# The add of the down product to x, per token tile: one operation of 1024 columns in place of two of 512

## What is computed

```python
def layer_tail(x, o_a, o_b, lp):
    o = jnp.concatenate([rmsnorm(o_a, lp['out_norm_a']), rmsnorm(o_b, lp['out_norm_b'])], axis=-1)
    x = x + o @ lp['w_out']
    h = rmsnorm(x, lp['norm2_g'])
    return x + (jax.nn.silu(h @ lp['w_gate']) * (h @ lp['w_up'])) @ lp['w_down']
```

## Time and profile before

| | |
|---|---|
| timed runs, median of 3 | 1887.27 us (1881.82 to 1888.38) |
| the profiled execution | 1884.58 us |
| its span, first to last instruction | 1882.6 us |
| TensorE busy | 1776.3 us, 94% |
| VectorE busy | 728.5 us, 39% |
| ScalarE busy | 390.3 us, 21% |
| GpSimd busy | 273.5 us, 15% |
| L1923, adds of the down product | 396 operations, 251.7 us |
| DMA | 94.73 MB, mean 50 GB/s |

### The profile page before, as it was taken

The page is one execution under the profiler, slowest core; times in us unless marked ns, Lnnn a source line. Parts: engine busy times, 40 slices in busy tenths (PEclk is TensorE's granted clock), DMA queues, the critical chain, the costliest instruction groups (busy, mean ns, idle before and its releaser), DMA issues.

```text
span 1882.6 us, 25099 instructions
## 1 busy us (share of the span) xinstructions
PE 1776.3 (94%) x9317; PEld 1356.1 (72%) x9317; DVE 728.5 (39%) x1319; ACT 390.3 (21%) x862; POOL 273.5 (15%) x286
## 2 busy tenths in 40 slices
PE   7999999698778899999999899999999999999996
PEld 4464454587346666687776698998998998998894
DVE  2100334222224444574565215335335334334437
ACT  2100111122112323332332222112112112112112
POOL 2210121211300000000000113113113112112112
PEclk9999999698967999999999999999999999999999
DMA  8220100533630000000000121211211211211202
GB/s 294 78 89 0 45 1 6 141 90 109 188 107 4 4 4 1 4 4 1 4 1 1 34 68 34 68 33 33 67 33 33 67 33 33 67 33 33 67 11 90
DMA packets 91320, 94.73 MB, mean 50 GB/s; under 512 B 6353, under 2 KB 74546, under 8 KB 91154
## 3 DMA queue, kind: packets, MB, share of 16 engines
q1 hardware_dynamic: 69410, 73.99, 12.8%
q0 software_dynamic: 4240, 11.32, 2.0%
q10 hardware_dynamic: 17600, 8.47, 1.7%
HBM read 86.61 MB, written 11.34 MB: 52 GB/s over the span
## 4 chain that ended last, share of the span: by engine, by line
PE 86%; DVE 5%; issue 3%; DMA 2%; ACT 1%; SPq 1%; ACTq 1%; POOL 0%; POOLq 0%; DVEq 0%
PE bankpair L338 14%; PE bankpair L1793 9%; PE bankpair L1795 9%; PE bankpair L1794 9%; PE bankpair L1452 7%; PE bankpair L1421 6%; PE bankpair L1820 5%; PE bankpair L1511 5%; PE bankpair L1821 5%; PE bankpair L1822 5%; PE bankpair L819 3%; PE bankpair L1490 2%; DMA work<-in_state_win_kv 1%; PE bankpair L1408 1%; PE bankpair L803 1%
## 5 line engine op out<-in xcount | busy, mean ns | idle before, releaser
L1793 PE MATMUL bankpair<-h2T_high,w_high 128*128 128x344 f32 x1056 | 337.9, 320 | 0.0
L1795 PE MATMUL bankpair<-h2T_high,w_low 128*128 128x344 f32 x1056 | 337.1, 319 | 0.0
L1794 PE MATMUL bankpair<-h2T_low,w_high 128*128 128x344 f32 x1056 | 337.1, 319 | 0.0
L338 PE MATMUL bankpair<-work 128*128 128x512 f32 (+3 forms) x720 | 288.2, 557 | 0.8 <-DMA work<-in_w_in 0.8
L1923 DVE TENSOR_TENSOR x_all<-x_all,bankpair 128x512 f32<-128x512 f32 (+1 forms) x396 | 251.7, 684 | 1.7
L338 PEld LDWEIGHTS bankpair<-work 128*128 128x128 f32 (+1 forms) x720 | 127.2, 180 | 145.5 <-issue 136.6
L1909 DVE TENSOR_TENSOR kT_space<-kT_space,bankpair 128x344 f32<-128x344 f32 x66 | 33.9, 513 | 451.4 <-ACT kT_space L1857 451.4
L1793 PEld LDWEIGHTS bankpair<-h2T_high,w_high 128*128 128x128 f32 x1056 | 198.6, 188 | 3.1 <-issue 0.2
L1794 PEld LDWEIGHTS bankpair<-h2T_low,w_high 128*128 128x128 f32 x1056 | 198.1, 188 | 1.1 <-issue 0.2
L1795 PEld LDWEIGHTS bankpair<-h2T_high,w_low 128*128 128x128 f32 x1056 | 198.4, 188 | 0.0
L1844 POOL TENSOR_TENSOR w_low<-work,w_high 128x1024 fp32r<-128x1024 f32 x44 | 105.5, 2421 | 565.5 <-ACT w_high L1839 565.5
(11 more groups left out here) (270 smaller groups left out, 2064.3 us busy)
## 6 DMA issues: line engine op xcount, KB each, us to landing
work<-in_w_gate SPq DMA_DIRECT2D x22, 512.0 KB, 5.0
work<-in_w_up SPq DMA_DIRECT2D x22, 512.0 KB, 6.2
work<-in_w_down SPq DMA_DIRECT2D x22, 512.0 KB, 3.8
work<-in_w_in SPq DMA_DIRECT2D x4, 2048.0 KB, 7.9
x_all<-in_x_prompt SPq DMA_DIRECT2D x8, 512.0 KB, 12.2
work<-in_cache_kv_cmp SPq DMA_DIRECT2D x32, 128.0 KB, 2.8
work<-in_cache_kv_cmp POOLq DMA_DIRECT2D x32, 128.0 KB, 2.9
work<-in_cache_kv_slc POOLq DMA_DIRECT2D x32, 128.0 KB, 3.7
```

The source lines that it names most:

```text
L338: ins = pe.matmul(pb(at_n % 4)[0:n, 0:w], hT[:, k, P * t:P * t + n], wslot[c % 2][:, k, 0:w], start=(k == 0), stop=(k == KD - 1))
L1793: pe.matmul(out, wh, high, start=(k == 0), stop=False)
L1794: pe.matmul(out, wh, low, start=False, stop=False)
L1795: ins = pe.matmul(out, wl, high, start=False, stop=(k == KD - 1))
```

## The change

```diff
--- before.py
+++ after.py
@@ -1812,8 +1812,8 @@
                 n = rows(t)
                 ah, al = (a[s][:, P * t:P * t + n] for a in (act_high, act_low))
                 for half in range(2):
-                    if not (first and j == 0 and t < 2):
-                        pe.wait_ge(y_added, j * YH + (2 * t + half - 3))
+                    if half == 0 and not (first and j == 0 and t < 2):
+                        pe.wait_ge(y_added, j * XT + (t - 1))
                     cols = slice(512 * half, 512 * half + 512)
                     out = bank[2 + (s + t) % 2][0:n, cols]
                     wh, wl = w_high[s][2][:, 0, cols], w_low[s][2][:, 0, cols]
@@ -1878,7 +1878,7 @@
         step(NJ - 1, 1, last=True)
         for t in range(XT):
             n = rows(t)
-            act.wait_ge(y_added, (NJ - 1) * YH + 2 * t + 2)
+            act.wait_ge(y_added, (NJ - 1) * XT + t + 1)
             if t:
                 act.wait_ge(y_squared, t)
             act.activation(sq_y[0:n, :], x_all[0:n, t, :], ACT.Square, accum_out=ssf[0:n, t:t + 1]).then_inc(y_squared, 1)
@@ -1915,12 +1915,11 @@
 
         def add_tile(j, s, t, first):
             n = rows(t)
-            for half in range(2):
-                x = x_all[0:n, t, 512 * half:512 * half + 512]
-                dve.wait_ge(y_ready, j * YH + (2 * t + half + 1))
-                if not first:
-                    dve.wait_ge(y_added, j * YH + (2 * t + half + 1 - YH))
-                dve.tensor_tensor(x, x, bank[2 + (s + t) % 2][0:n, 512 * half:512 * half + 512], ALU.add).then_inc(y_added, 1)
+            x = x_all[0:n, t, :]
+            dve.wait_ge(y_ready, j * YH + (2 * t + 2))
+            if not first:
+                dve.wait_ge(y_added, j * XT + (t + 1 - XT))
+            dve.tensor_tensor(x, x, bank[2 + (s + t) % 2][0:n, :], ALU.add).then_inc(y_added, 1)
 
         def add(j, s, first=False):
             for t in range(XT):
```

## The result

The changed kernel takes 1911.51 us (median of 4 runs, 1906.58 to 1919.31), the kernel before 1884.90 (median of 4 beside them, 1881.82 to 1888.38). The ratio is 1.0144, with a 95% interval of 1.0103 to 1.0186: slower, by 27 us. The profiled execution has a span of 1908.1 us, before 1882.6.

The account below looks back on a forecast made before the run. TensorE was taken as the bound. 20 products at +1.31, +1.04 in product 0 and about +0.1 in the last gave +27.3 us on 1887.27, forecast as 1914.5 us; range 1898 to 1922.

Parts of the forecast that it names:

- The bound: Whole kernel: TensorE, busy 94% of the span, bounds it; whatever delays it in a down product lengthens the kernel.
- The long add: VectorE's 1024-column add: lasts 1.221 us, following each other after about 1.135, against 1.195 for two halves.
- The first wait: Tile 2 of each down product: TensorE starts at 3.57 instead of 2.79 us, losing 0.78 where 0.25 was lost.
- The new waits: Tiles 4, 6 and 8 of a down product: loop of 1.66 us against 1.395, so 0.26 lost at each.
- The room before the change: Down products of the kernel before: each add frees its half 0.7 us before needed, so no second TensorE wait.
- Tiles 3, 5 and 7: In each down product: they lose nothing, since the shift made by the wait before them is just enough.
- Product 0: Down product j = 0, written out: hand-over 0.04, so 0.17 lost three times; 1.04 us more than before.
- The last product: Product j = 21, VectorE-bound: 2.33 us per tile instead of 2.39, first norm chain 0.54 later; about +0.1 us.
- only the first wait grows: Rival, down products: weight loads run ahead and absorb the 0.26 waits; +11.1 us, 1898.5 us; chance 0.10.
- Faster by saved overhead: Rival, wait at tile 2: VectorE's 0.06 us per tile shortens it, at most 5.2 us; 1881.6 us; chance 0.03.
- The clock: Rival, down products: granted clock falls to 0.50, 12.6 us per product; four of 21 give 1965 us; chance 0.04.

Follow-up runs that it names:

- tensor_whole: Kernel before, adds still 512 wide, but TensorE waits for a whole tile, at the tile's first half; 1.0067 of the kernel before.
- three_places_long: The change's 1024-column adds, with three PSUM places for the down product, gate and up of a chunk sharing one bankpair; 0.9970 of the kernel before.
- early_long: The change with two low parts (L1913) of the next step made after all adds of the product, so adds begin sooner; 1.0104 of the kernel before.
- early_short: Kernel before, adds of 512, with two low parts (L1913) of the next step made after the add of tile 4; 1.0146 of the kernel before.

## Why the prediction was right, point by point

**The bound.** TensorE sets the end, and what it waits for lengthens the kernel one to one: the periods of the down products account for all but about 0.2 us of the 25.6 that the stretch grew.

**The long add.** Forecast 1.221 long and 1.135 from start to start; 1.219, and two in 2.34, so 1.12 to 1.13.

**The first wait.** Forecast 0.78 lost at tile 2; 0.79.

**The new waits.** Forecast 0.26 at tiles 4, 6 and 8. Tiles 4 and 6 lose 0.26 to 0.29, tile 8 only 0.17. Here a term was mis-sized. I took 0.15 for the hand-over back to TensorE at every tile. It contains the loading of 128 columns of weights, and tile 8 has 8 rows, so 8 columns: in the loads' timeline its load starts at 1435.28 and its matmul at 1435.29.

```profile
1435.28 0.09 PEld L1820 LDWEIGHTS bankpair<-w_high,act_high 128*8 128x8 f32 x1 [0.44 <-DVE x_all L1922]
```

That is 0.1 less in each of 21 products, 2 us, and covers the difference between +27.3 and +25.6; the last product takes a little back. The sum per product was 1.56, the measured one 1.48 as the mean over products 0 to 20.

**The room before the change.** The prediction says that each add of the kernel before frees its half 0.7 us before it is needed. Its own rows give less at first: the second half of tile 2 can start at 2.20 + 0.60 + 0.68 + 0.15 = 3.63 and is due at 2.79 + 0.25 + 0.70 = 3.74, 0.11 later. The room grows by 0.1 with each half, the difference between 0.698 and 0.598, and is near 1 us at the end. No term of the sum uses the 0.7. But the small room shows why TensorE's wait for a whole tile alone costs so much: its first half was needed at 2.79, and comes with the second at 3.63.

**Tiles 3, 5 and 7.** They lose no matmul time, as forecast, but the loads of tiles 5 and 7 do wait. So the loads wait six times per product, 126 in all, where I had announced some 80. The loads' timeline of the changed kernel at tiles 2, 4 and 5 (idle before each in brackets):

```profile
1426.08 0.19 PEld L1820 LDWEIGHTS bankpair<-w_high,act_high 128*128 128x128 f32 x1 [0.95 <-DVE x_all L1922]
...
1429.14 0.19 PEld L1820 LDWEIGHTS bankpair<-w_high,act_high 128*128 128x128 f32 x1 [0.45 <-DVE x_all L1922]
...
1430.53 0.19 PEld L1820 LDWEIGHTS bankpair<-w_high,act_high 128*128 128x128 f32 x1 [0.15 <-DVE x_all L1922]
```

The idle time of 0.95 at tile 2 is the 0.9 that the prediction names. The 0.15 at tile 5 is inside the load's lead over its matmul, which starts at 1430.66, one step after 1430.43, and costs nothing. The count of waits misled; the matmul starts were the right measure.

**Product 0.** Forecast +1.04; it starts at 1129.48 and product 1 at 1165.86, 36.38 apart, +0.93.

**The last product.** Forecast +0.1 from its first matmul on; from 1876.98 to the end are 31.1 us, before from 1851.72 to the end 30.9. The pace is the one forecast, 2.33 per tile, and the first norm is late as forecast. VectorE in the last product:

```profile
1882.08 1.29 DVE L1933 SCALAR_TENSOR_TENSOR work<-x_all,small,norm_g 128x1024 f32<-128x1024 f32 x1 [0.79 <-POOL small L207]
1883.28 1.21 DVE L1922 TENSOR_TENSOR x_all<-x_all,bankpair 128x1024 f32<-128x1024 f32 x1
1884.41 1.27 DVE L1933 SCALAR_TENSOR_TENSOR work<-x_all,small,norm_g 128x1024 f32<-128x1024 f32 x1
1885.61 1.21 DVE L1922 TENSOR_TENSOR x_all<-x_all,bankpair 128x1024 f32<-128x1024 f32 x1
1886.74 1.27 DVE L1933 SCALAR_TENSOR_TENSOR work<-x_all,small,norm_g 128x1024 f32<-128x1024 f32 x1
```

1882.08 is 5.10 after the product's first matmul, 4.42 before (1856.14 in the earlier trace rows): 0.68 later, forecast 0.54. Of the rest, 0.08 is a small wait at the product's start, where the second matmul comes 0.31 after the first and not 0.23; the code there waits for the add of tile 7 of product 20. Another 0.05 is the hand-over to the first add, forecast 0.04 and measured 0.09.

**The rivals.** That only the first wait grows would have given `tensor_whole`'s time; the change is 13.5 us above it in the stretch. Faster by saved overhead: the saving is real and visible where VectorE is the bound (2.33 against 2.39 per tile in the last product) and is lost elsewhere. The clock stayed at 1.00 in the whole stretch, although TensorE paused four times per product. The Trainium skill (TensorE: Matmul & The Clock Gate, A second HAM failure mode: psum-queue depth-cycling) tells of short idles between groups of matmuls that made the clock swing; this trace does not show it for waits of 0.17 to 0.79 us.

**The time.** Forecast 1914.5 on the footing of three runs with a median of 1887.27; measured 1911.51 beside 1884.90. That is +27.3 forecast, +26.6 between the medians and +25.6 in the stretch of the profiled executions. The timed runs of the change alone lie 12.7 us apart, so they can't tell these three from each other; the rows of the single product can.

## What to carry to other kernels

Merging two operations saves their overhead only on the engine that runs them; where their buffer is handed back to a busier engine, ask first how long the buffer is held. With two places, compare hand-over + operation + hand-over back with the producer's time for one place (here 0.285 + 1.22 + 0.15 against 1.395); if it is longer, each second place waits. A third place removed these waits with the operation as it was (`three_places_long`), and so did a release by halves or a shorter operation. An earlier start took 0.5 us off the first wait of a product and left the others (`early_long`). When an operation is moved in its queue, look at what the other engines do at its new time: its old duration may not hold there.

## What the runs showed of the hardware

**VectorE beside GpSimd.** An operation of VectorE whose two inputs both lie in SBUF (L1912 of `early_short`, 128x344) did not run beside a GpSimd subtraction. It started 0.41 us after it and took 2.37 in place of 0.51, up to 0.36 after GpSimd's end; over products 0 to 19 this happened every time. The adds of `x_all` and a bankpair, one input in PSUM, take 0.69 beside GpSimd operations (118 of them in `early_short`) and 0.67 to 0.69 without. The Trainium skill (SBUF — State Buffer, SBUF: two separate sides) says that such an operation and a GpSimd one share a pair of ports, which the first to start holds for its whole length. These rows agree, down to the waiting for the end; that ports are the cause no run here shows.

**Hand-overs have a size, and it depends on where the wait stands.** From the end of a matmul to the add 0.04 us where the add itself waits and 0.13 where a register instruction in a loop waits ahead of it (0.09 at the first add behind the loop); from the end of an add to the load of weights 0.05, and 0.10 more until the matmul counts, which a load of 8 columns does not need.
